# A hybrid attention and DeltaNet block on one core: VectorE splits weights two quarters behind ScalarE, and GpSimd substitutes before it issues the next pair's decay transfers

## What is computed

```python
proj = h @ w_in + b_in                       # 2048 x 14880, cut into q/k/v, gates and so on
o_att = sliding_window_sink_attention(aq, ak, av, att_sinks)
o_dn = gated_rms_norm(gated_delta_rule_chunked(q, k, v, g, beta), dz, dn_norm_g)
merged = sigmoid(ga) * (o_att @ w_br_att) + sigmoid(gb) * (o_dn @ w_br_dn)
h = layer_norm(ALPHA * h + merged @ w_out, ln_mix_g, ln_mix_b)
ffn = (silu(h @ w_gate) * (h @ w_up)) @ w_down
ple = sigmoid(h @ w_ple_gate + b_ple_gate) * (p @ w_ple_proj)
out = layer_norm(ALPHA * h + ffn + ple, ln_ffn_g, ln_ffn_b)
```

## Time and profile before

| what | value |
|---|---|
| median of 3 runs | 1907.46 us (1907.27 to 1907.67) |
| the profiled execution | 1907.71 us, of which the span of instructions is 1905.9 us |
| mean granted TensorE clock | 0.998 of full speed |
| TensorE matmuls busy | 1887.0 us (99% of the span) |
| VectorE busy | 1250.8 us (66%) |
| ScalarE busy | 1039.5 us (55%) |
| GpSimd busy | 105.6 us (6%) |
| mean DMA rate | 183 GB/s |
| a mixer turn | 62 us, of which matmuls busy 61.3 us in turns 2 to 7 |

### The profile page before, as it was taken

One profiled execution on the slowest core, in us unless ns is written; L12 is line 12 of the kernel. 1 busy time (PEld: TensorE's weight loads), 2 busy tenths in 40 slices (PEclk: granted clock), 3 DMA queues, 4 the chain that ended last, 5 costly groups with the idle time before them and its releaser, 6 DMA issues.

```text
span 1905.9 us, 27743 instructions
## 1 busy us (share of the span) xinstructions
PE 1887.0 (99%) x9497; PEld 1585.5 (83%) x9497; DVE 1250.8 (66%) x2189; ACT 1039.5 (55%) x2108; POOL 105.6 (6%) x208
## 2 busy tenths in 40 slices
PE   9999999999999999999999999999999999999997
PEld 8888888888888888888888788888888888888886
DVE  6658888898888665655666776555555555545555
ACT  4447776667767554555444655544444445444442
POOL 2001022111220100000000000000000000000000
PEclk9999999999999999999999999999999999999999
DMA  8666565555654657665565465556555555665552
GB/s 318 208 157 179 149 146 138 116 165 130 151 132 142 193 189 248 198 199 190 195 245 181 152 219 199 190 185 197 181 194 189 186 183 191 224 207 189 196 199 89
DMA packets 204180, 349.63 MB, mean 183 GB/s; under 512 B 6768, under 2 KB 73024, under 8 KB 203088
## 3 DMA queue, kind: packets, MB, share of 16 engines
q1 hardware_dynamic: 200704, 334.00, 52.7%
q0 software_dynamic: 3264, 14.47, 5.6%
q10 hardware_dynamic: 144, 0.26, 0.0%
HBM read 344.32 MB, written 2.10 MB: 182 GB/s over the span
## 4 chain that ended last, share of the span: by engine, by line
PE 83%; DVE 9%; issue 4%; POOL 2%; ACT 2%; DMA 1%; DVEq 1%; ACTq 0%; POOLq 0%; SPq 0%
PE dense L658 23%; PE dense L660 23%; PE dense L659 23%; PE dense L646 5%; PE dense L648 3%; DVE lo L1518 2%; DMA raw<-in_w_in_dram 1%; POOL less L571 1%; POOL sub L574 1%; PE chain L822 1%; PE chain L1104 1%; DVE pad L1689 0%; DVE qd L1814 0%; PE chain L924 0%; PE chain L916 0%
## 5 line engine op out<-in xcount | busy, mean ns | idle before, releaser
L1518 DVE TENSOR_TENSOR lo<-raw,hi 128x512 fp32r<-128x512 f32 x1252 | 843.0, 691 | 427.2 <-ACT hi L1154 423.8
L1154 ACT ACTIVATE hi<-raw 128x512 fp32r<-128x512 f32 x1252 | 777.0, 630 | 632.3 <-PE dense L660 611.5
L658 PE MATMUL dense<-hi,xs 128*128 128x512 f32 x1376 | 540.0, 392 | 1.8 <-DVE xs L2081 1.1
L660 PE MATMUL dense<-lo,xs 128*128 128x512 f32 x1376 | 536.2, 390 | 0.0
L659 PE MATMUL dense<-hi,xs 128*128 128x512 f32 x1376 | 535.9, 389 | 0.0
L646 PE MATMUL dense<-xs,hi 128*128 128x512 f32 x1024 | 379.9, 410 | 0.0
L658 PEld LDWEIGHTS dense<-hi,xs 128*128 128x128 f32 x1376 | 258.4, 188 | 55.8 <-DVE xs L2081 2.0
L660 PEld LDWEIGHTS dense<-lo,xs 128*128 128x128 f32 x1376 | 258.4, 188 | 53.9
L659 PEld LDWEIGHTS dense<-hi,xs 128*128 128x128 f32 x1376 | 258.5, 188 | 52.4
L648 PE MATMUL dense<-xs,lo 128*128 128x256 f32 x1024 | 286.3, 280 | 0.0
L646 PEld LDWEIGHTS dense<-xs,hi 128*128 128x128 f32 x1024 | 192.5, 188 | 42.9 <-DVE lo L1518 3.1
(11 more groups left out here) (327 smaller groups left out, 1435.7 us busy)
## 6 DMA issues: line engine op xcount, KB each, us to landing
raw<-in_w_in_dram SPq DMA_DIRECT2D x115, 1024.0 KB, 5.1
raw<-in_w_ffn_gate_dram SPq DMA_DIRECT2D x44, 1024.0 KB, 5.1
raw<-in_w_ffn_up_dram SPq DMA_DIRECT2D x44, 1024.0 KB, 5.1
raw<-in_w_ffn_down_dram SPq DMA_DIRECT2D x44, 1024.0 KB, 5.0
raw<-in_w_br_att_dram SPq DMA_DIRECT2D x16, 1024.0 KB, 5.1
raw<-in_w_br_dn_dram SPq DMA_DIRECT2D x16, 1024.0 KB, 5.0
raw<-in_w_out_dram SPq DMA_DIRECT2D x16, 1024.0 KB, 5.1
raw<-in_w_ple_gate_dram SPq DMA_DIRECT2D x16, 1024.0 KB, 5.0
```

The costliest lines, as they stand in the source:

```text
L658: pe.matmul(o, ah, hi[:, s, :], start=(k == 0), stop=False)
L660: mm = pe.matmul(o, ah, lo[:, s, :], start=False, stop=(k == nk - 1))
L1154: act.activation(parts(pos, n)[0], raw[:, slot, off:off + 512], ACT.Copy).then_inc(sem("hi_ready"), 1)
L1518: dve.tensor_tensor(wl, raw[:, slot, off:off + 512], wh.bitcast(F32), ALU.subtract).then_inc(sem("lo_ready"), 1)
```

## The change

There are four edits. VectorE's distance `BEHIND` becomes 4 in place of 5, while ScalarE's `LEAD` stays 6. On GpSimd, `back_rows(p)` stands ahead of the issue of the next decay transfers. On ScalarE the copy to `blk` gets a function of its own, `rows_copy`, and stands ahead of the chain's other work of quarter 2. On ScalarE the exponential of `Em` moves from quarter 12 to quarter 26 of the turn.

```diff
-BEHIND = 5
+BEHIND = 4
@@ gpsimd
             for p in range(PAIRS):
                 power_of("length", "k_eps", row[:, 1, :], row[:, 4, :], p)
+                back_rows(p)
                 if p + 1 < PAIRS:
                     pool.wait_ge(sem("egb"), p + 1)
                     pool.wait_ge(sem("am"), p + 1)
                     decay_in(p + 1)
-                back_rows(p)
-                if p + 1 < PAIRS:
                     causal(p + 1)
                     unit_blocks(p + 1)
                     power_of("rms", "o_eps", row[:, 8, :], row[:, 9, :], p)
@@ scalar
-                if k == 12:
+                if k == 26:
                     act.wait_ge(sem("am"), i + 1)
...
+            def rows_copy(p):
+
+                act.wait_ge(sem("x_prod"), nth("x_prod", 0, p))
+                act.activation(blk[:].rearrange("p x i j -> p (x i j)"), C[:, 0, 0:256], ACT.Copy).then_inc(sem("vu_out"), 1)
+
             def inverse_k(k, p):


-                if k == 5:
-                    act.wait_ge(sem("x_prod"), nth("x_prod", 0, p))
-                    act.activation(blk[:].rearrange("p x i j -> p (x i j)"), C[:, 0, 0:256],
-                                   ACT.Copy).then_inc(sem("vu_out"), 1)
-                elif k in (9, 11, 13):
+                if k in (9, 11, 13):
...
                     split(pos, k)
                     if chain:
+                        if copy_at(k) == 5:
+                            rows_copy(i - 1)
                         chain_k(stage_at(k), i - 1)
```

More of the change, by code:

```diff
@@ L1405, in _ @@
                     chain_k(stage_at(LAST_AT[n]), PAIRS - 1)
+                    if copy_at(LAST_AT[n]) == 5:
+                        rows_copy(PAIRS - 1)
                     inverse_k(copy_at(LAST_AT[n]), PAIRS - 1)
```

## The result

The changed kernel takes 1913.62 us (median of 6 runs, 1913.16 to 1916.23), the kernel before in the same comparison 1907.68 (6 runs, 1907.27 to 1907.90). The ratio is 1.0034 with a 95% interval of [1.0023, 1.0045]: 5.9 us slower, where 4.4 were forecast. The profiled execution of the changed kernel took 1913.90 us, its span is 1912.1 against 1905.9 before.

The account below looks back on a forecast made before the run. TensorE was taken as the bound, busy 1887.0 of 1905.9 us. Terms -0.8 (set-up), -1.5 (L822), +3.2 (L842), +3.24 (PLE), +0.25 (feed-forward) sum to +4.4, forecasting 1911.8 us, range 1906.8 to 1914.5.

Parts of the forecast that it names:

- Set-up, -0.8: Set-up: quarter 20 leaves the queue ahead of `krow`, so TensorE's wait at L741 goes, -0.8 us.
- L822, -1.5: Mixer: substitution starting sooner shortens TensorE's wait for `Ym` by 0.25 us in six turns, -1.5 us.
- L842, +3.2: Mixer: the later mask blocks a VectorE split, delaying TensorE's matmul on `Yz` in seven turns, +3.2 us.
- PLE, +3.24: PLE gate quarters: splits behind the low part and `unit_rows` delay TensorE in a loop over three engines, +3.24 us.
- rival B: PLE: TensorE waits 0.93 us once and catches up through hidden slack, total 1909.5 us; chance 0.1.
- Feed-forward start, +0.25: Start of the feed-forward groups: quarter 4, now behind `ple_add(3)`, comes late for TensorE, +0.25 us.
- Edit 4 and the copy at nothing: ScalarE: exponential at quarter 26 and earlier copy to `blk` cost nothing; without idle cover the exponential costs up to 1 us a turn.
- Rival A: Mixer: the mask lands on VectorE work it doesn't block, total 1906.5 to 1908.5 us; chance 0.27.
- A2: Mixer: both TensorE waits, L822 and L842, vanish, -6.2 us there, total 1903.7 us; chance 0.06.
- C: Mixer: the mask's block also holds L1765 and L842 moves by 0.9 us a turn, total 1914.5; chance 0.12.
- D: Mixer: decay transfers take over 25 us, so the exponential waits at quarter 26, costing microseconds a turn; chance 0.02.
- The band of 0.2%: Whole kernel: a measurement can't tell less than about 0.2% (3.8 us) from no change.

Follow-up runs that it names:

- mask late: Changed kernel with GpSimd's mask (L588) behind `unit_blocks`: 1908.72 us, ratio 1.0004 to the kernel before.
- mask that reads nothing: Changed kernel with the mask's addition at L588 replaced by three memsets of `Em`, mask and decay values left out: 1909.03 us, ratio 1.0005 to the kernel before.
- the moves alone: Changed kernel with BEHIND back at 5, leaving only the moves on GpSimd and ScalarE: 1913.58 us, ratio 1.0030 to the kernel before.
- PLE mended: Changed kernel with VectorE's split ahead of the block's low part in PLE's first 16 steps: 1910.06 us, ratio 1.0011 to the kernel before.
- quarter 0 mended: Changed kernel with only PLE's gate quarter 0 split ahead of block 0's low part: 1913.04 us, ratio 1.0022 to the kernel before.
- BEHIND 4 mended: Kernel before with BEHIND 4, PLE's first 16 splits ahead of the low part, first feed-forward split ahead of `ple_add(3)`, no moves: 1907.42 us, ratio 0.9997.
- all mended: Changed kernel with mask behind `unit_blocks`, PLE's splits ahead of the low part, first feed-forward split ahead of `ple_add(3)`: 1903.89 us, ratio 0.9978 to the kernel before.

## Why the prediction was right, step by step

The time came out 1.8 us above the forecast and inside its range, on the side that had 0.47. No error hid another: the small terms were near, the two large ones both too small (L842 by 1.0, PLE by 0.4), and 0.57 of the profiled execution is the program's start, which no term had. The steps:

- **Set-up, -0.8.** It was -0.85. `krow` started at 34.73 and not at 34.2, since all of this execution was 0.57 late from the program's start. `dbT` was ready at 40.55, 0.95 before L740 started at 41.50.
- **L822, -1.5.** It was -1.6, six times 0.24 to 0.31. The reason given held: the substitution began 0.8 sooner, but one more of its operations fell into VectorE's row of splits (five of 0.57 to 0.67 instead of four). What the copy to `blk` and the order on GpSimd each gave of it wasn't run apart.
- **L842, +3.2.** Right mechanism, wrong size: +4.2. The terms written down, 0.5 in six turns and 0.4 in turn 1, add up to 3.4 already, so the forecast was 0.2 too low by a slip. The place of the mask was met to a hundredth. The split behind it lost 0.83 (1.52 less 0.69) where I took 0.7. The credit of 0.2 was real: TensorE came to L822 0.43 sooner than before, and L1769 started 0.64 sooner than L1765 had, 0.21 more. 0.83 less 0.21 is 0.62, and L842 moved by 0.67 a turn, not 0.5. The last 0.05 I can't place. Turn 1 gave 0.14 and not 0.4, because there the mask had run for 0.84 us when the split began, and not for 0.32. Experiments with the mask late and with a mask that reads nothing take the whole of it away.
- **PLE, +3.24.** It was +3.6: 1.01, 0.92, 0.87, 0.09, 0.54, 0.18 against my 0.93, 0.83, 0.83, 0, 0.5, 0.15. Each term is 0.03 to 0.09 larger. The loop, read from start to start, takes 7.31 (quarter 0 to 4) and 7.29 (4 to 8) where I had 7.26. Where the difference is spent I didn't test. The runs with all quarters and with quarter 0 alone ahead show that it is a loop, not one wait: rival B is out.
- **Feed-forward start, +0.25.** It was 0.36: 0.25 at the first matmul, and 0.11 at the second, which stands 0.34 behind the first instead of 0.23.
- **Edit 4 and the copy at nothing.** Right in the changed kernel, where the old place would have cost nothing either. But I named only the idle time ahead of L1257 as its cover. The cover that matters is `BEHIND` 4: with 5, the exponential at quarter 26 costs 2 us in jumps at L781, and 3.3 us between the medians. The edits are not additive. BEHIND 4 alone is +4.3 us, the moves alone +5.5, and both together +5.9.
- **What no step had.** A wait of 2.1 us, some 2.5 us behind one of 0.5, after which the clock falls in some executions, at a cost of 1.5 to 1.6 us. In five profiled executions with that wait it fell in four (BEHIND 4 alone, mask late, mask that reads nothing, exponential at 12) and didn't in the changed kernel's own. In the six profiles without it (the moves alone, with either place of the exponential, PLE mended, quarter 0 mended, BEHIND 4 mended, all mended), and in that of the kernel before, it stayed at its upper level from the trace's first record of it to the program's last ten microseconds. The two slower runs of the changed kernel would fit a fall, but they have no trace, so this stays an inference. A warning stands beside it: of the 21 executions of the kernel before that were compared with the last two kernels (quarter 0 ahead, and BEHIND 5 with the exponential at 12), three took 1910.9 to 1911.5 us, at a mean granted clock of 0.997 where the others have 0.998 or 0.999. They have no trace either, but they show that a lower mean clock, and a loss of 3 us, also comes in a kernel whose trace has no wait of 2.1 us. What decides in which execution it falls is open.

Rival A is out: the operation under the mask was a split with two inputs. A2 and C are out by the turn's own sum of +0.4, and D because ScalarE's exponential (L1236) never waited for the mask in the changed kernel. The band of 0.2% was too wide: the intervals measured here reach 0.09 to 0.12% to each side.

## What to carry to other kernels

Filling a ring one step later was free here wherever the filler was far enough ahead, in the mixer's turns too, and cost time only where work stood between two fills and the reader was close behind. Where those fills were part of a loop over three engines, it cost time in each round. Look up those places and put the fill first there, rather than judge the distance as a whole: here two such places cost 4.0 us, and with them and the mask's place mended the same change was a gain.

When work on GpSimd is moved, follow its last instruction, not its first: the substitution's gain of 0.27 us a turn was paid for by a mask that slid seven microseconds down the turn onto a two-input instruction of VectorE. And measure a pair of edits as a pair. One of them may be the cover of the other.

## What the runs showed of the hardware that I had not expected

- TensorE's granted clock can fall to 1.2 GHz after a wait of 2.1 us that follows one of 0.5. In four traces it fell 0.2 to 1.2 us after work had begun again, and stayed there for some eight matmuls of 512 columns (0.63 us each instead of 0.39, starts 0.43 apart instead of 0.23). Where the longest wait there was 1.0 to 1.1 us no profile shows a fall.
- A VectorE instruction that GpSimd blocks doesn't end when the other ends. The mask ended at 266.80 and the split that had been waiting at 267.35, so the split needed 0.55 us of its own 0.69 after the release. What it loses is less than the overlap: 0.83 us of 0.97 there, 0.30 of 0.45 in turn 1, and in turn 1 of the two kernels with `BEHIND` 5 0.68 of 0.81 and 0.32 of 0.47. That is 0.13 to 0.15 less each time.
- TensorE's clock rises at a different time in each execution, and this moves a span by up to 1.5 us without any edit. The first matmuls of the program (128 columns) stand 0.21 us apart, then 0.11. The change comes where the trace's first record of the clock at 2.4 GHz begins: at 4.89 us in the kernel before, 6.10 in the changed one, 4.20 with the moves alone and 7.42 with quarter 0 ahead. Ahead of that record the profile has none, and the windows view shows 1.00 there; the doubled distances, as 0.43 for 0.23 at the fall above, say that the clock was at its lower level. TensorE had been at work since 1.25 us in all of them.
